# Latent-attention products placed between the projection tiles of the neighbourhood heads, on one Trainium2 core

## The reference

```python
def even_mixer(a_lat, a_ctx, ...):
    p_lat = a_lat @ w_in                       # w_in: 1024 x (256 + 128 + 32 + 3 * 512)
    p_ctx = a_ctx @ w_in
    # latent attention (MLA), 8 heads of 64 + 32:
    q     = rms_norm(p[:, :256], q_norm) @ w_q_up          # last 32 of each head rotated (latent tokens)
    c_kv  = rms_norm(p[:, 256:384], kv_norm)
    k     = [c_kv @ w_uk (per head), rotate(p[:, 384:416])]
    v     = c_kv @ w_uv
    # neighbourhood attention (NA), 8 heads of 64:
    q, k, v = p[:, 416:].reshape(3, 8, 64); latent scores get rel_bias
    return concat(o_mla, o_na) @ w_out
```

## Time and profile before

| | us |
|---|---|
| Median of the 3 runs shown | 2402.71 |
| Lowest and highest of them | 2401.49, 2403.73 |
| The profiled execution's own time | 2398.93 |
| Its span in the profile | 2397.1 |
| PE busy | 2277.6 (95%) |
| DVE busy | 1019.2 (43%) |
| ACT busy | 495.6 (21%) |
| Mean granted TensorE clock | 0.976 of full |

### The profile page before, as it was taken

One profiled execution on the slowest core, in us unless ns is written; L12 is line 12 of the kernel. 1 busy time (PEld: TensorE's weight loads), 2 busy tenths in 40 slices (PEclk: granted clock), 3 DMA queues, 4 the chain that ended last, 5 costly groups with the idle time before them and its releaser, 6 DMA issues.

```text
span 2397.1 us, 42253 instructions
## 1 busy us (share of the span) xinstructions
PE 2277.6 (95%) x17824; PEld 1580.9 (66%) x17824; DVE 1019.2 (43%) x2159; ACT 495.6 (21%) x1057; POOL 0.2 (0%) x4
## 2 busy tenths in 40 slices
PE   6999899999998999999999979989999999799998
PEld 4554456999986444444444437658888887688997
DVE  2046757444413222222223047444444642547785
ACT  4010242332212111111111026410111001341111
POOL 0000000000000000000000000000000000000000
PEclk9999999999998999999999989999999999999999
DMA  9266688000163999999981210012222223113441
GB/s 362 86 268 237 259 358 316 22 4 4 55 248 147 412 422 422 422 422 422 422 330 47 70 70 2 19 71 88 88 88 88 88 88 110 36 54 138 163 176 54
DMA packets 59036, 430.18 MB, mean 179 GB/s; under 512 B 6528, under 2 KB 6784, under 8 KB 7296
## 3 DMA queue, kind: packets, MB, share of 16 engines
q1 hardware_dynamic: 57168, 416.31, 44.1%
q10 hardware_dynamic: 1712, 11.58, 1.3%
HBM read 426.81 MB, written 1.05 MB: 178 GB/s over the span
## 4 chain that ended last, share of the span: by engine, by line
PE 90%; DVE 6%; DMA 2%; ACT 1%; issue 1%; ACTq 0%; DVEq 0%
PE bank L565 87%; PE bank L713 2%; DMA ring<-in_w 1%; DVE normed L1720 1%; DMA arena<-in_xin 0%; DVE small L1756 0%; PE bank L1234 0%; DVE arena L1789 0%; DVE arena L1788 0%; DVE arena L1845 0%; PE bank L1243 0%; PE bank L609 0%; DVE normed L1739 0%; ACT arena L1544 0%; DVE arena L1787 0%
## 5 line engine op out<-in xcount | busy, mean ns | idle before, releaser
L565 PE MATMUL bank<-arena 64*64 64x64 f32 (+8 forms) x9512 | 927.9, 293 | 23.5 <-DVEq L506 13.6
L565 PEld LDWEIGHTS bank<-arena 64*64 64x64 f32 (+4 forms) x9512 | 681.3, 153 | 223.2 <-issue 175.0
L565 PE MATMUL bank<-normed,ring 128*128 128x256 f32 (+2 forms) x2048 | 562.0, 431 | 12.0 <-DVE normed L1739 5.5
L565 PEld LDWEIGHTS bank<-normed,ring 128*128 128x128 f32 x2048 | 368.4, 195 | 193.4 <-issue 150.5
L565 PE MATMUL bank<-arena,ring 128*128 128x256 f32 (+1 forms) x1104 | 206.9, 338 | 4.1 <-DVE arena L2328 3.6
L565 PE MATMUL bank<-ring,arena 128*64 128x512 f32 (+1 forms) x1008 | 206.2, 599 | 4.4 <-DMA ring<-in_w 2.2
L565 PEld LDWEIGHTS bank<-arena,ring 128*128 128x128 f32 x1104 | 177.9, 191 | 21.9 <-DVE arena L2328 4.2
L565 PEld LDWEIGHTS bank<-ring,arena 128*64 128x64 f32 (+1 forms) x1008 | 62.7, 132 | 133.5 <-issue 116.4
L2161 DVE TENSOR_TENSOR arena<-arena,bank 128x512 f32<-128x512 f32 x72 | 49.5, 687 | 136.9 <-PE bank L565 136.8
L1639 ACT ACTIVATE arena<-arena 128x256 f32<-128x256 f32 (+1 forms) x88 | 32.0, 363 | 342.0 <-DVE arena L2325 216.6
L1756 DVE TENSOR_REDUCE small<-bank 128x1 f32<-128x512 f32 (+1 forms) x112 | 63.8, 609 | 38.6 <-PE bank L565 38.5
(11 more groups left out here) (335 smaller groups left out, 1793.4 us busy)
## 6 DMA issues: line engine op xcount, KB each, us to landing
ring<-in_w SPq DMA_DIRECT2D x298, 1024.0 KB, 8.5
arena<-in_w SPq DMA_DIRECT2D x99, 1024.0 KB, 13.4
arena<-in_xin ACTq DMA_DIRECT2D x1, 2048.0 KB, 9.0
arena<-in_nab ACTq DMA_DIRECT2D x1, 2048.0 KB, 11.6
con<-in_con ACTq DMA_DIRECT2D x1, 1472.5 KB, 14.4
sw<-in_sw ACTq DMA_DIRECT2D x1, 1280.0 KB, 5.7
sw<-in_sw ACTq DMA_DIRECT2D x1, 1168.0 KB, 20.2
arena<-in_xin ACTq DMA_DIRECT2D x1, 1024.0 KB, 4.8
```

Source lines behind the costliest of these rows:

```text
L565: return nc.tensor.matmul(o, l, r, start=start, stop=stop, **kw)
```

## The change

The squares, the root of the key latents and the temporary of the rotation get places in `arena` (columns 14336 to 16895) that nothing holds between the n3 sums and the relative bias, in place of parts of `osb`. With that the MLA part no longer has to stand behind the projections, and its steps are put between their output tiles. The barrier that stood ahead of it goes, so that the later ones are numbered one lower. The bias is requested behind the one barrier that is left ahead of the attention. On DVE the rotation of `krt` comes first, ahead of the two reciprocals.

```diff
+        sq_q, mla_rk, rot_t = region(14336, 1536, "p (x t) -> p x t", x=3), region(15872, 512), region(16384, 512)
 # PE
             project(4, slice(0, T), "dve", "n3")
-            project(8, slice(0, T), "act")
-            project_tok("act")
-            phase(2)
-            pe.wait_ge(S("small_in"), 32)
+            project(1, slice(0, T), "act")
             marks["mla"] = dict(gave)
             pe.wait_ge(S("mla_sq"), 2)
             (first sum, of sq_q instead of osb)
             pe.wait_ge(S("mla_sq"), 3)
             (second sum)
-            pe.wait_ge(S("mla_normed"), 3)
+            pe.wait_ge(back["dve"], marks["proj2"]["dve"] + 4)
+            j = job("dve")
+            last = mm(banks[j[0]][:, 0:SEQ], C("perm32"), krt[:, LAT], True, True)
+            done(j, last)
+            project(2, slice(0, T), "act")
+            pe.wait_ge(S("small_in"), 32)
+            pe.wait_ge(S("mla_normed"), 2)
             for h in range(8):   (query heads)
-            (permutation of krt)
             up = dict(gave)
+            pe.wait_ge(S("mla_normed"), 3)
+            project(1, slice(0, T), "act")
             for h in range(8):   (key heads)
             for g in range(4):   (permutations of the query rows)
+            project(1, slice(0, T), "act")
             for i in range(4):   (values)
+            project(3, slice(0, T), "act")
+            project_tok("act")
+            phase(2)
+            attention("even", even_pairs())
             phase(3)
-            attention("even", even_pairs())
-            phase(4)
             out_proj(lambda k: osb[:, k, :], T, "res_n4")
 # ACT
             modulate("n3", slice(0, T), mod2a[:, 0:16])
-            copies(4, lambda j: naq[:, j, :], 64 ** -0.5)
-            copies(4, lambda j: nak[:, j, :])
-            copies(4, lambda i: nav[:, i, :])
-            barrier(a, "", 2)
-            act.dma_start(arena[:, 14336:18432], dram["nab"]).then_inc(S("bias_in"), 16)
             for x in range(3):
+                act.wait_ge(back["dve"], marks["proj2"]["dve"] + x + 1)
-                a.signals(f(osb[:, 4 + x, :], src, ACT.Square), "mla_sq")
+                a.signals(f(sq_q[:, x, :], src, ACT.Square), "mla_sq")
+            copies(1, lambda j: naq[:, 0, :], 64 ** -0.5)
             (two roots; the second into mla_rk)
+            copies(2, lambda j: naq[:, 1 + j, :], 64 ** -0.5)
             (four query heads)
+            copies(1, lambda j: naq[:, 3, :], 64 ** -0.5)
             (eight key heads)
+            copies(1, lambda j: nak[:, 0, :])
             (four value tiles)
+            copies(3, lambda j: nak[:, 1 + j, :])
+            copies(4, lambda i: nav[:, i, :])
+            barrier(a, "", 2)
+            act.dma_start(arena[:, 14336:18432], dram["nab"]).then_inc(S("bias_in"), 16)
+            attention("even", even_pairs())
             barrier(a, "", 3)
 # DVE
             (four copies of pq, ckv, krt)
-            barrier(v, "", 2)
-            rq, rk = rs_t, osb[:, 7, :]
+            rotate(krt[:, LAT], C("cos32"), C("sin32"), rot_t[:, 0:SEQ])
+            rq, rk = rs_t, mla_rk
             (reciprocal, two scalings, reciprocal, scaling, four query heads)
-            rotate(krt[:, LAT], C("cos32"), C("sin32"), osb[:, 6, 0:SEQ])
             (copy of the key rows, four rotations with rot_t)
+            barrier(v, "", 2)
+            attention("even", even_pairs())
             barrier(v, "", 3)
```

More of the change, by code:

```diff
@@ L1277, in _ @@
             j = job("act")
-            mm(banks[j[0]][:, :], ones, osb[:, 4, :], True, False)
-            last = mm(banks[j[0]][:, :], ones, osb[:, 5, :], False, True)
+            mm(banks[j[0]][:, :], ones, sq_q[:, 0, :], True, False)
+            last = mm(banks[j[0]][:, :], ones, sq_q[:, 1, :], False, True)
             done(j, last)
@@ L1282, in _ @@
             j = job("act")
-            last = mm(banks[j[0]][:, :], ones, osb[:, 6, :], True, True)
+            last = mm(banks[j[0]][:, :], ones, sq_q[:, 2, :], True, True)
             done(j, last)
-            pe.wait_ge(S("mla_normed"), 3)
+            pe.wait_ge(back["dve"], marks["proj2"]["dve"] + 4)
[5 more added lines that the diff above has]
+            pe.wait_ge(S("mla_normed"), 2)
             for h in range(8):
@@ L1291, in _ @@
                 done(j, last)
-            j = job("dve")
-            last = mm(banks[j[0]][:, 0:SEQ], C("perm32"), krt[:, LAT], True, True)
-            done(j, last)
             up = dict(gave)
+            pe.wait_ge(S("mla_normed"), 3)
+            project(1, slice(0, T), "act")
             for h in range(8):
@@ L1335, in _ @@
             drained()
-            phase(5)
+            phase(4)
             attention("swa", swa_pairs())
@@ L1602, in _ @@
             modulate("n3", slice(0, T), mod2a[:, 0:16])
-            copies(4, lambda j: naq[:, j, :], 64 ** -0.5)
-            copies(4, lambda j: nak[:, j, :])
+            for x in range(3):
+                act.wait_ge(back["dve"], marks["proj2"]["dve"] + x + 1)
+                src = pq[:, x, :] if x < 2 else ckv
+                a.signals(f(sq_q[:, x, :], src, ACT.Square), "mla_sq")
+            copies(1, lambda j: naq[:, 0, :], 64 ** -0.5)
+            for x in range(2):
+                b = a.take()
+                a.gives(f(mla_rk if x else rs_t[:, :], b[:, :], ACT.Sqrt, bias=eps_c[:, 0:1],
+                          scale=1.0 / (256 if x == 0 else 128)))
+            copies(2, lambda j: naq[:, 1 + j, :], 64 ** -0.5)
+            for h in range(0, 8, 2):
+                b = a.take()
+                a.given(f(qf[0:96, h, :], b[0:96, :], ACT.Copy, scale=96 ** -0.5))
+            copies(1, lambda j: naq[:, 3, :], 64 ** -0.5)
+            for h in range(8):
+                b = a.take()
+                a.given(f(kf[0:64, h, :], b[0:64, :], ACT.Copy))
+            copies(1, lambda j: nak[:, 0, :])
+            for i in range(4):
+                b = a.take()
+                a.given(f(mv[:, i, :], b[:, :], ACT.Copy))
+            copies(3, lambda j: nak[:, 1 + j, :])
             copies(4, lambda i: nav[:, i, :])
@@ L1607, in _ @@
             act.dma_start(arena[:, 14336:18432], dram["nab"]).then_inc(S("bias_in"), 16)
-            for x in range(3):
-                src = pq[:, x, :] if x < 2 else ckv
-                a.signals(f(osb[:, 4 + x, :], src, ACT.Square), "mla_sq")
[L1611 to L1623, removed]
+            attention("even", even_pairs())
             barrier(a, "", 3)
-            attention("even", even_pairs())
-            barrier(a, "", 4)
             norm("n4", sq_b, slice(0, T), after="res_n4")
@@ L1648, in _ @@
             copies(1, lambda j: region(2560, 512))
-            barrier(a, "", 5)
+            barrier(a, "", 4)
             attention("swa", swa_pairs())
@@ L2215, in _ @@
                 rotate(qf[R32, 2 * g:2 * g + 2, LAT], turn(C("cos32")), turn(C("sin32")),
-                       osb[R32, 6, :].rearrange("p (h t) -> p h t", h=2), rows=R32)
+                       rot_t[R32, :].rearrange("p (h t) -> p h t", h=2), rows=R32)
+            barrier(v, "", 2)
+            attention("even", even_pairs())
             barrier(v, "", 3)
-            attention("even", even_pairs())
-            barrier(v, "", 4)
             residual(mod2a, 2, slice(0, T))
@@ L2337, in _ @@
             v.does(ts(negsink, Q("sinks", 0, 16), -1.0, None, MUL))
-            barrier(v, "", 5)
+            barrier(v, "", 4)
             attention("swa", swa_pairs())
```

## The result

The changed kernel took 2382.7 us (median of 4 runs, 2381.51 to 2384.63), the one before beside it 2402.1 (4 runs, 2398.01 to 2403.73). The ratio is 0.9927 with a 95% interval of 0.9915 to 0.9938, that is 17.5 us less (14.9 to 20.4); the two medians lie 19.4 us apart, inside that interval. Timed again in two later sets, the unchanged pair gave 0.9935 (0.9921 to 0.9949) and 0.9925 (0.9912 to 0.9937). The range was 2384.5 to 2392.3. The profiled execution took 2383.5 us, 15.4 less than the profiled one before.

What follows compares the result with a forecast made beforehand. PE was taken as the bound, busy 2277.6 of 2397.1 us. The terms summed to 145.8 us from first projection to first score against 159.6, so 2402.7 - 13.8 = 2388.9 us; range 2384.5 to 2392.3.

Steps and rivals of the forecast that it cites:

- Steps 1 to 5: PE stream before the attention: projections 111.8 us, sums 2.6, query heads 13.8, permutations with key heads 11.1, values 3.4.
- Step 6: Projection tile behind the four 32x32 permutations: runs at low clock, costing 1.8 us, bounds 0 and 3.6.
- rival A: Behind the 32x32 permutations: no low clock, so 15.6 us less, 2387.1 us; chance 0.22.
- Step 7: Barrier ahead of the attention: PE waits 0.75 us for ACT's copy of a value tile, against 1.06 before.
- Step 8: Changes of form between kinds of product on PE: some five new switches cost 0.5 us, bounds 0 and 1.
- What must hide: Work under PE's projections and attention: `pq` chain ready with 7 us margin, `ckv` 17, bias landing 36 us cover.
- B: Ahead of the query heads: DVE's chain is late; half the hole staying gives 2393.5 us, all 2398; chance 0.08.
- C: At the ten new seams: ACT or DVE hold PE, 1.4 us each, no gain, 2402.7 us; chance 0.03.
- D: At the nineteenth pair: bias comes late, each us of landing beyond 48 costs one, slower kernel; chance 0.02.

Runs made afterwards that it cites:

- before_again: The kernel before, unchanged, profiled a second time; 0.9989 of before, stage 161.1 us.
- heads_uncovered: The changed kernel with both projection tiles ahead of the query heads moved behind them; 2397.1 us, 0.9977 of before.
- bias_late: The changed kernel with the bias requested by ACT behind its work on the eighteenth pair instead of ahead of the first; 2394.88 us, 0.9967 of before.
- after_narrow_twice: The changed kernel with each of the four 32x32 permutations issued twice into the same bank; 2390.43 us, 0.9946 of before.
- rotations_sooner: The kernel with only the chain and `krt` rotation early, other MLA products behind all projections, its permutations moved ahead of the key heads; 0.9934 of before.

## Why the prediction was too small

**Steps 1 to 5, the stream.** Right. Query heads 13.73 us start to start (13.8), sums and `krt` permutation 3.01 (3.1), values 3.43 (3.4), all projections together 112.0 (111.8).

**Step 6, the low clock behind the narrow products (1.8 us).** This is the step that failed, in two ways. It did not come in any of the seven profiled executions in which a projection tile stands behind the four permutations, so the term is 0 (rival A, given 0.22). Where something else stands behind them it came in two of four, and so few cases do not show that the tile is what kept it away. And it was not a cost in the kernel before: I read the slow values and the wait of 1.06 us at the barrier as two separate things. before_again shows them as one, 10.0 us fixed by DVE. The rotations on DVE were the bound there, and the low clock only filled PE's wait. Freed of them, the same two groups and the barrier take 3.55 + 3.43 + 0.73 = 7.7 us, 2.3 us less, where I had 0.3 at the barrier. The view that would have told it was in hand: the chain of before, shown under before_again, leaves PE for DVE's steps, and I used it for the holes alone.

**Step 7, the barrier.** 0.73 us, released by ACT's copy, as forecast (0.75).

**Step 8, the seams.** Taken as 0.5 us, measured as good as 0 in the sum. A switch does show: the two tiles that stand alone take 6.96 and 6.97 us for 16 x 0.43 = 6.88, and the projections in all 0.2 us more than before. But the sums, the query heads and the `krt` permutation came out 0.2 us under their prices.

Steps 6 and 8 are the 2.3 us between 145.8 and 143.5. The rest of the distance between 13.8 and 17.5 us lies within the interval of the measurement, to which the holes of before add their own spread: with before_again as the one before, the stage alone gives 161.1 - 143.5 = 17.6 us.

**What must hide.** Right at each place and within 0.2 us for the chain; heads_uncovered and bias_late put prices on both covers. What I undersized there is what a hole costs at the clock behind it: 1.7 us in the earlier trace rows, but 2.65 behind 6.44 us in heads_uncovered and 3.0 behind 7.06 us in bias_late. The request of the bias ahead of the first exponential was priced at nothing; it brought 0.6 us (last section).

**The rivals.** A held in every profile of the changed kernel. B, C and D did not happen. A's 15.6 us less lies inside the measured interval, where the forecast's 13.8 does not. The range was narrow at its low end, as it left only 2 to 3 us below A's time of 2387.1.

## What to carry to other kernels

When PE waits at a barrier, look at which engine reached it last and how long its own work ran: a slow stretch of PE just ahead of such a wait can be slack and not cost, and is then not to be counted beside it. A short chain on another engine (root, reciprocal, scaling) is hidden best by giving it independent products that were to be done anyway; moving the chain alone early, with the products that need it left behind, brought 14 of the 16 us here, and a cover of twice its length held. A transfer may be moved late as long as its landing time ends before its first user, and the trace gives both numbers; past that point PE loses the wait and the slow clock behind it.

## What was not expected of the hardware

The granted clock fell from 1.00 to 0.50 while PE was busy, during or just behind a run of 32x32 products: in 2 of 11 profiled executions with 3.6 us of them, and in the one with 9.3 us. In before PE had been busy for 27 us when it fell, in after_narrow_twice for over 80; in rotations_sooner there was a pause of 0.98 us just ahead of the narrow products. The sentence of the Trainium skill weighed in step 6 (TensorE: Matmul & The Clock Gate, "Part 1: The HAM clock gate") explains a drop by idling, and the drops of before and after_narrow_twice had none; where page and rows differ, the rows decide. Why only some executions show it was not settled.

From the first score product to the first bias product it is 49.3 us before and 48.7 after, with the same instructions. The difference is the wait of 0.65 us at the first transposes, and it hangs on ACT: the table load of the first exponential starts 0.78 us behind the first score product after, 1.38 before. bias_late, with the barrier in place and only the request of the bias taken away from there, has the late load and the wait again. The load in the changed kernel, then load and transposes in bias_late:

```profile
1421.71 1.28 ACT L1431 ACT_TABLE_LOAD   x1 [0.88 <-PE bank L566]
```

```profile
1422.70 1.28 ACT L1431 ACT_TABLE_LOAD   x1 [1.52 <-DVE small L1770]
...
1425.65 0.70 PE L714 MATMUL bank<-con,arena 128*128 128x128 f32 x4 [0.66 <-DVE arena L1792]
```

With the request directly ahead of it the load starts before DVE has the first maximum; without it, 0.15 us behind that. In all profiles with the barrier and the request behind it the load comes 0.75 to 0.78 us behind the first score product, in the four without such a request (the three of before, and bias_late) 1.38 to 1.43. Without the barrier the request itself comes 0.88 us behind the first score, the load at 1.31, and the wait is there. So the gain of 0.6 us in the attention is an effect of where the bias is requested. What in the request lets the load start sooner was not tried.
